# Eleven modulation tiles moved from the value panels to the down projection of the gating mixer

## The reference

```python
cond = jax.nn.silu(c)
mod = cond @ ada_w[i] + ada_b[i]
sh1, sc1, g1, sh2, sc2, g2 = jnp.split(mod, 6, axis=-1)
h = rms_norm(x, norm_mix[i]) * (1.0 + sc1) + sh1
y = chunked_spatial_gating(h, ...)          # second layer
x = x + g1 * y
h = rms_norm(x, norm_ffn[i]) * (1.0 + sc2) + sh2
x = x + g2 * squared_relu_mlp(h, ffn_w1[i], ffn_w2[i])

# chunked_spatial_gating
z = jax.nn.gelu(h @ w_in, approximate=False)
u, v = jnp.split(z, 2, axis=-1)             # 3072 columns each
v = rms_norm(v, v_gain)                     # needs all 3072 columns of v
vm = einsum(w, v) + b_s                     # mixes positions in windows of 128
return (u * vm) @ w_out
```

## Time and profile before

| | us |
|---|---|
| median of 3 runs (1946.93 to 1951.79) | 1947.72 |
| the profiled execution's own time | 1941.69 |
| its span in the trace | 1939.9 |
| TensorE busy | 1823.2 (94%) |
| VectorE busy | 1154.1 (59%) |
| mean granted TensorE clock | 0.978 of full |

### The profile page before, as it was taken

One profiled execution on the slowest core, in us unless ns is written; L12 is line 12 of the kernel. 1 busy time (PEld: TensorE's weight loads), 2 busy tenths in 40 slices (PEclk: granted clock), 3 DMA queues, 4 the chain that ended last, 5 costly groups with the idle time before them and its releaser, 6 DMA issues.

```text
span 1939.9 us, 24528 instructions
## 1 busy us (share of the span) xinstructions
PE 1823.2 (94%) x9449; PEld 1525.6 (79%) x9449; DVE 1154.1 (59%) x2392; ACT 669.9 (35%) x1086; POOL 101.9 (5%) x198
## 2 busy tenths in 40 slices
PE   3999999999999999998999999999999998999669
PEld 3887767988888887777888898888888877777657
DVE  5776565686557656556444448864776587445442
ACT  3323564432232334223232335232323422655120
POOL 0001110000000100110000000010001100000000
PEclk9999999999999999999999999999999999999789
DMA  8444331244533525662222224463436223102501
GB/s 334 142 148 153 105 109 55 104 142 109 204 109 120 183 70 186 226 217 87 87 87 102 73 87 148 141 198 122 145 120 195 98 87 130 44 23 90 204 22 65
DMA packets 44400, 246.00 MB, mean 127 GB/s; under 512 B 6080, under 2 KB 6304, under 8 KB 25728
## 3 DMA queue, kind: packets, MB, share of 16 engines
q1 hardware_dynamic: 23200, 153.26, 22.2%
q0 software_dynamic: 21088, 91.21, 14.2%
HBM read 229.23 MB, written 15.22 MB: 126 GB/s over the span
## 4 chain that ended last, share of the span: by engine, by line
PE 80%; DVE 11%; DMA 4%; ACT 2%; issue 2%; SPq 0%; DVEq 0%; ACTq 0%
PE ps L465 66%; DMA ada_raw<-in_ada 3%; DVE w_lo L1384 3%; PE ps L636 2%; PE ps L657 2%; PE ps L901 2%; PE ps L646 1%; DMA ada_first<-in_ada 1%; DVE ada_raw L1412 1%; PE ps L775 1%; PE ps L882 1%; PE ps L891 1%; ACT w_hi L971 1%; PE ps L939 1%; PE ps L927 1%
## 5 line engine op out<-in xcount | busy, mean ns | idle before, releaser
L1384 DVE TENSOR_TENSOR w_lo<-w_raw,w_hi 128x2048 fp32r<-128x2048 f32 x136 | 311.6, 2291 | 149.4 <-ACT w_hi L971 149.1
L971 ACT ACTIVATE w_hi<-w_raw 128x2048 fp32r<-128x2048 f32 x136 | 260.1, 1913 | 399.3 <-PE ps L465 376.8
L465 PE MATMUL ps<-h_hi,w_hi 128*128 128x512 f32 (+1 forms) x1008 | 379.8, 377 | 14.6 <-issue 5.1
L465 PE MATMUL ps<-h_lo,w_hi 128*128 128x512 f32 (+1 forms) x1008 | 375.0, 372 | 0.0
L465 PE MATMUL ps<-h_hi,w_lo 128*128 128x512 f32 (+1 forms) x1008 | 374.9, 372 | 0.0
L465 PEld LDWEIGHTS ps<-h_hi,w_hi 128*128 128x128 f32 x1008 | 192.7, 191 | 48.4 <-issue 9.3
L465 PEld LDWEIGHTS ps<-h_hi,w_lo 128*128 128x128 f32 x1008 | 192.2, 191 | 32.7
L465 PEld LDWEIGHTS ps<-h_lo,w_hi 128*128 128x128 f32 x1008 | 192.7, 191 | 30.9
L465 PE MATMUL ps<-hid_hi,w_hi 128*128 128x512 f32 (+1 forms) x576 | 211.3, 367 | 0.0
L465 PE MATMUL ps<-hid_hi,w_lo 128*128 128x512 f32 (+1 forms) x576 | 210.6, 366 | 0.0
L465 PE MATMUL ps<-hid_lo,w_hi 128*128 128x512 f32 (+1 forms) x576 | 210.5, 366 | 0.0
(11 more groups left out here) (377 smaller groups left out, 2532.1 us busy)
## 6 DMA issues: line engine op xcount, KB each, us to landing
w_raw<-in_slabs SPq DMA_DIRECT2D x136, 1024.0 KB, 4.8
ada_raw<-in_ada POOLq DMA_DIRECT2D x108, 512.0 KB, 4.5
s_tables<-s_tab POOLq DMA_DIRECT2D x4, 2692.0 KB, 9.5
s_t<-s_tables POOLq DMA_DIRECT2D x4, 2692.0 KB, 9.8
ada_first<-in_ada SPq DMA_DIRECT2D x4, 1536.0 KB, 18.3
a_bias<-in_a_bias POOLq DMA_DIRECT2D x16, 256.0 KB, 3.0
xT<-in_xT SPq DMA_DIRECT2D x1, 2048.0 KB, 20.0
s_toeplitz<-KTp POOLq DMA_DIRECT2D x32, 64.0 KB, 3.3
```

The lines of the kernel that those rows point to most:

```text
L465: last = mm(o, l, r, start=start and n == 0, stop=stop and n == 2)
L971: A(w_hi[s][:], w_raw[:, s, :], ACT.Copy).then_inc(sem("hi_done"), 1)
L1384: tt(w_lo[s][:], w_raw[:, s, :], w_hi[s][:].bitcast(F32), ALU.subtract).then_inc(sem("lo_done"), 1)
```

## The change

Before, the value panels 1 to 5 hold 6, 6, 7, 6 and 7 tiles (64 to 95). After, they hold 4, 4, 5, 4 and 4 (64 to 84). The other eleven follow one in each slab: four in the down projection of chunk 0, four in chunk 1, three in the tail. A put stands behind each of the three. The number of tiles, of loads and of matmuls is the same; VectorE executes three more puts, six instead of three.

```diff
-ADA_BV = 0, 6, 6, 7, 6, 7
+ADA_BV = 0, 4, 4, 5, 4, 4
...
-                (tail if ch == CHUNKS - 1 else residual)(64)
+                (tail if ch == CHUNKS - 1 else residual)(64, lambda s: ada(1, 0))
+                ada_put()
```

## The result

The changed kernel is faster. Its median is 1930.83 us (1929.81 to 1932.59, 5 runs), beside 1946.93 us (1942.66 to 1951.79, 5 runs) for the kernel before on the same chip. The ratio is 0.9918 with a 95% interval of 0.9899 to 0.9937, which is 16.1 us less, between 12.3 and 19.7. The profiled execution took 1930.01 us with a span of 1928.2, against 1941.69 and 1939.9 before.

The account below looks back on a forecast made before the run. TensorE, 80% of the chain, waits in the value panels for splits queued on VectorE behind tiles awaiting loads. 10.66 + 5.01 - 0.2 - 2.9 = 12.6 us won, so 1947.72 - 12.6 = 1935.1 us, range 1930 to 1940.

Parts of the forecast that it names:

- The panels' 10.66 us: Panels 2, 3 and 4 take 2.15, 0.71 and 7.80 us over the 21.76 without waits; all 10.66 us are won.
- Four and five tiles: Panels with four tiles cause no wait, 3.3 us left at the longest first load; panel 3's five wait 0 to 0.5.
- The term of 0.2 us for panel 3's fifth tile: Wait at panel 3's second split: 1.3 us early by panel 5's load times, 0.5 late by panel 3's; 0.2 taken.
- Behind the last panel: From the fourth gelu's start (mark) to the first mixing matmul 9.45 us instead of 14.46, 5.01 won; TensorE idles 4.0.
- the sum: Gain of 10.66 + 5.01 - 0.2 - 2.9 = 12.6 us over panels, last panel, fifth tile and clock.
- The clock: Lower clock behind the new 4.0 us idle stretch costs 2.9 us behind the mixing, bounds 0 and 4.
- The rival by which less is lost to the clock: Clock doesn't fall in the new gap, or for less work: up to 2.9 us more won, 1932.2 us; chance 0.15.
- The new places: Eleven tiles of 1.23 us in down projection and tail slabs cost nothing; tail's third slab bound 0 to 1.3 us.
- The slower rival: A tile lands over 20 us after issue, TensorE waits at down projection slabs: 3.9 us slower, 1951.6 us; chance 0.02.
- The rivals of the loads and of giving back: Loads still hold panels: 1939.1 us, chance 0.13. Gain lost later to the clock's steps: 1944 us and up, chance 0.07.
- The step from the sum to the median: Profiled execution lies 6.0 us under the three runs' median; distance kept, so 1947.72 - 12.6 = 1935.1 us.
- the clock rival: Clock doesn't fall in the new gap, or for less work: 15.5 us won, 1932.2 us; chance 0.15.

Follow-up runs that it names:

- e3: Kernel before with all 32 tiles in the panels, but tiles 66 to 95 not loaded, VectorE multiplying the condition by itself there; 1928.84 us against 1942.74, ratio 0.9935.
- e9: Kernel before with its counts and loads, but a panel's tiles over four put behind its second split; 1937.98 us against 1945.73, ratio 0.9963.
- e2: Kernel after, but the last panel has its seven tiles again and the tail none; 1935.19 us against 1942.74 for the kernel before, ratio 0.9959.
- e1: Kernel after, but panels 1 to 4 keep their old tile counts, only the last panel has four; 1939.06 us against 1942.74 for the kernel before, ratio 0.9977.
- e8: Kernel before, unedited, profiled once more; 208.68 us from panel 1's fourth gelu to chunk 1's first mixing matmul, 206.57 in the first trace.
- e6: Kernel after, but each of the eleven moved tiles is multiplied four times instead of once; one execution of 1932.7 us, span 1930.9.
- e5: Kernel after, but panels 1 to 4 hold five tiles each and the tail none; one execution of 1928.69 us beside 1945.64 for the kernel before.
- e4: Kernel after, but both half slabs of the first u slab come ahead of both mixing groups; 1922.45 us against 1942.74 for the kernel before, ratio 0.9899.
- e7: Kernel before, unedited, profiled again; 205.43 us from panel 1's fourth gelu to chunk 1's first mixing matmul, 206.57 in the first trace.
- e10: Kernel after, unchanged, run again beside the kernel before on one chip; 1928.78 us against 1945.73, ratio 0.9917.
- e11: Kernel after with both half slabs of the first u slab ahead of the mixing, run again; 1920.46 us, ratio 0.9878 to the kernel before.

## Why the prediction was right, step by step

**The panels' 10.66 us.** Right, and shown from two sides: without the loads (e3) and with the loads but the split ahead of the late tiles (e9) the excess is 0, as in the kernel after. The size belongs to one trace. Two more gave 8.31 and 11.36.

**Four and five tiles.** Four leave no wait, as forecast. The term of 0.2 us for panel 3's fifth tile measured 0: the two waits for loads were 4.25 and 2.84 us and the split was 1.6 us early, nearer to the 1.3 of panel 5's times than to the 0.5 late of panel 3's. The Trainium skill's estimate from "DMA: Bandwidth & Descriptors", "Anatomy of one DMA", also gave 0 here, but not for the reason: the landings took 3.7 to 6.3 us, not 3.2.

**Behind the last panel.** Predicted 9.45 us from mark to mixing, 5.01 us won and one wait of 4.0 us for `b_v`. Measured 9.52, 4.94 and 4.1. But e2 shows that this term and the first are not independent, as the sum treats them. The last panel alone gave its 4.94 us (e1). The first panels alone gave 7.5 us instead of 10.66, since from the fifth mark to the mixing it then took 3.1 us more than before. The sum was right because both were made. Nor did the prediction name the third load of panel 5, of 3.79 us, though the wait of 4.07 hung on it.

**The clock.** The mechanism was right and the term was mis-sized: 2.9 us predicted, 1.64 measured. It was taken from the one gap of 4.07 us. In e8 a gap of 4.08 us at the same place cost 1.71. At the new place six traces have the gap of 4.1 us: it cost 1.60 to 1.64 in five of them (the kernel after twice, e1, e3 and e6) and 2.72 in e5. So one such row gives a value out of a spread, and 2.86 was at its top. The rival by which less is lost to the clock was partly the case.

**The new places.** Predicted 0, measured 0, the tail's third slab too. The slower rival, a tile that lands late in the down projection, needed over 20 us; the longest landing there was 7.7 and no tile was waited for.

**The rivals of the loads and of giving back.** The loads do not hold the panels; even five tiles in four panels (e5) leave the marks at 21.76. On giving back: the last mixing group starts at 1119.67 us before (span 1939.9) and here in the kernel after, on its timeline of TensorE:

```profile
1104.98 1.05 PE L775 MATMUL ps<-b_ws,b_v 128*128 128x128 f32 x8
```

To the end that is 820.2 us before and 823.2 after. So 3.0 of 14 us seem given back. A stretch of the kernel after shows a place:

```profile
1610.00:1620.00 10.00, 10.00 (x36) 7.68 (x36) 3.68 (x4) 0.31 (x1) 0.00 (x0) 0.78 0.50 195
```

and the kernel before, 14.7 us later, where the same work runs:

```profile
1624.70:1634.70 10.00, 10.00 (x43) 7.92 (x42) 3.60 (x4) 0.31 (x1) 0.00 (x0) 0.94 0.51 193
```

The lower clock lasted longer after, 0.78 against 0.94. But the other runs show no price of the change. On each chip the traces with all tiles in the panels take about as long there as those with moved tiles: 823.4 us (e3) beside 824.1, 823.5 and 822.5 (e1, e2, e4); 826.6 and 826.5 (e7, e8) beside 824.6 (e5) and 826.6 (e6, with 2.7 at its own norm); 823.8 (e9) beside 823.3 (e10) and 824.8 (e11). The 820.2 us of the first trace are the lowest of all. So the forecast that nothing links the change to it holds as far as these traces go.

**The step from the sum to the median.** This is the step that was off. The sum was 12.6 us, and 14.0 were measured in the stage between the first traces. The 1.4 us more are the 1.3 of the clock and the 0.2 of the fifth tile, less 0.07 behind the panel. To it I kept a distance of 6.0 us between the profiled execution and the median. The kernel after has 0.8 us there. The profiled execution of before was a low one: behind the last mixing group it was 2.3 us or more under every other trace, and some 6 us under its two repeats. The stage gives 12.8 to 16.1 us against the three traces of before, 14.3 in the mean, and the medians 16.1 and, in e10, 17.0. The some 2 us between lie within the interval; where they come from is left open. So 1930.83 us came out at the lower end of the range of 1930 to 1940, 4.3 us under the forecast of 1935.1 and nearer to the clock rival's 1932.2. The 1929.1 us for the profiled execution missed its 1930.01 by only 0.9, and that is luck: the gain was 2.1 us larger than the sum, and 3.0 us were lost in a part where the sum has nothing.

## What to carry to other kernels

A small wait for a load is dear when the engine that waits runs in order and something urgent is queued behind it: count from the mark to the urgent instruction, not the engine's busy time. Tiles that need a reload from two buffers belong one by one where each load has a whole stage to land, and not in a burst ahead of a split. Gains at neighbouring places of one chain may depend on each other, so test each alone before adding them up. And a second and third trace of the kernel before show which terms of a sum are stable: here the panel without waits was the same to about 0.01 us everywhere, while the excess differed by 3 us and the cost of a clock fall by 1.3.

## What the runs showed of the hardware that was not expected

The price of a clock fall does not follow from the length of the gap alone. Gaps of 4.1 us cost 1.60 to 1.64 us five times, 2.72 and, at the other place, 1.71 and 2.86, and the gap of 12.3 us of e9 cost (2.07 + 6.54) - (1.16 + 5.47) = 1.98. The loads of tiles in the down projection, each alone beside the slabs, landed in 5.2 us in the median, slower than the 3.8 of the first layer, though none was waited for. The same instructions behind the last mixing group took between 820.2 and 826.6 us in three traces of one kernel, and the record does not say whether they ran on one chip. And panel 1's mark, ahead of which nothing was changed, stood between 768.67 us (e11) and 775.82 (e10) on one chip.
